# Seams of the first block: sums of squares as columns of 128 tokens by four instead of rows

## The reference

```python
def _rmsnorm(x, g):
    x32 = x.astype(jnp.float32)
    y = x32 * lax.rsqrt(jnp.mean(x32 * x32, axis=-1, keepdims=True) + EPS)
    return (y * g.astype(jnp.float32)).astype(x.dtype)

def _sublayer(x, fn, pre_g, post_g, shift, scale, gate, res_w):
    h = _rmsnorm(x, pre_g) * (1.0 + scale[:, None, :]) + shift[:, None, :]
    y = _rmsnorm(fn(h), post_g)
    return x + res_w * (1.0 + gate[:, None, :]) * y
```

## Time and profile before

| | |
|---|---|
| time, median of 3 runs | 3290.32 us (3289.46 to 3294.41) |
| the profiled execution: its time, its span | 3285.37 us, 3283.4 us |
| mean granted clock of TensorE in it | 0.974 of full speed |
| TensorE busy | 3067.9 us, 93% |
| VectorE busy | 1704.8 us, 52% |
| ScalarE busy | 1162.4 us, 35% |
| GpSimd busy | 1353.0 us, 41% |
| DMA | 365.34 MB, mean 111 GB/s |

### The profile page before, as it was taken

The page is one execution under the profiler, slowest core; times in us unless marked ns, Lnnn a source line. Parts: engine busy times, 40 slices in busy tenths (PEclk is TensorE's granted clock), DMA queues, the critical chain, the costliest instruction groups (busy, mean ns, idle before and its releaser), DMA issues. The chain is left out here.

```text
span 3283.4 us, 52437 instructions
## 1 busy us (share of the span) xinstructions
PE 3067.9 (93%) x20043; PEld 2472.1 (75%) x20043; DVE 1704.8 (52%) x3192; ACT 1162.4 (35%) x2085; POOL 1353.0 (41%) x895
## 2 busy tenths in 40 slices
PE   5999999899999999999999999998888899879997
PEld 4888876688887888877788888876666676668875
DVE  6444478654445575133774116446777756263343
ACT  3222234432223222234422224254454434343442
POOL 3444442344444434442434443245666630323332
PEclk8999999999999999999999999998999999979998
DMA  7665431255544654332354333123222233122221
GB/s 214 195 185 164 156 87 58 67 171 181 181 154 136 187 169 128 95 89 65 111 171 129 97 108 122 51 76 100 55 58 61 60 96 113 33 75 72 74 61 45
DMA packets 636933, 365.34 MB, mean 111 GB/s; under 512 B 107454, under 2 KB 629300, under 8 KB 636240
## 3 DMA queue, kind: packets, MB, share of 16 engines
q1 hardware_dynamic: 628944, 351.42, 36.2%
q10 hardware_dynamic: 6640, 10.49, 1.1%
q0 software_dynamic: 1168, 0.91, 0.1%
HBM read 333.67 MB, written 24.90 MB: 109 GB/s over the span
## 5 line engine op out<-in xcount | busy, mean ns | idle before, releaser
L270 POOL TENSOR_TENSOR w_lo<-w_raw,w_hi 128x1024 fp32r<-128x1024 f32 (+1 forms) x373 | 882.9, 2367 | 1568.3 <-ACT w_hi L262 1515.6
L262 ACT ACTIVATE w_hi<-w_raw 128x1024 fp32r<-128x1024 f32 (+1 forms) x372 | 386.8, 1040 | 946.1 <-PE acc L335 687.9
L335 PE MATMUL acc<-h,w_hi 128*128 128x512 f32 x2256 | 704.6, 393 | 0.0
L335 PEld LDWEIGHTS acc<-h,w_hi 128*128 128x128 f32 x2256 | 417.3, 188 | 84.8 <-issue 1.8
L335 PE MATMUL acc<-h,w_lo 128*128 128x512 f32 x1128 | 440.4, 390 | 0.0
L335 PE MATMUL acc<-hid,w_hi 128*128 128x512 f32 x1056 | 326.6, 390 | 0.0
L1005 DVE SCALAR_TENSOR_TENSOR ada_part<-ada_raw,c_act,ada_part 128x256 f32<-128x256 f32 x672 | 314.9, 488 | 18.6
L335 PE MATMUL lat<-h,w_hi 128*128 128x512 f32 x768 | 276.9, 403 | 16.7 <-DVE h L506 10.4
L335 PEld LDWEIGHTS acc<-h,w_lo 128*128 128x128 f32 x1128 | 211.7, 188 | 45.8
L335 PEld LDWEIGHTS acc<-hid,w_hi 128*128 128x128 f32 x1056 | 197.3, 188 | 40.7
L335 PE MATMUL spare<-h,w_hi 128*128 128x512 f32 x688 | 211.8, 389 | 0.0
(11 more groups left out here) (620 smaller groups left out, 5819.7 us busy)
## 6 DMA issues: line engine op xcount, KB each, us to landing
w_raw<-in_ffn_w SPq DMA_DIRECT2D x240, 512.0 KB, 4.0
ada_raw<-in_ada_w SPq DMA_DIRECT2D x88, 1024.0 KB, 5.0
w_raw<-in_od_w_in SPq DMA_DIRECT2D x32, 512.0 KB, 4.0
w_raw<-in_ffn_w SPq DMA_DIRECT2D x32, 384.0 KB, 3.2
w_raw<-in_ev_w_in SPq DMA_DIRECT2D x22, 512.0 KB, 3.9
image<-inverse_wait SPq DMA_DIRECT2D x144, 64.0 KB, 2.2
first_ada<-in_ada_w SPq DMA_DIRECT2D x8, 1024.0 KB, 12.5
w_raw<-in_ab_w_in SPq DMA_DIRECT2D x16, 512.0 KB, 4.0
```

Source lines behind the costliest of these rows:

```text
L262: act.activation(K.w_hi[:, first % SPLIT, 0:tiles, :], K.raw[:, first % RAW, 0:tiles, :], ACT.Copy).then_inc(K.hi_ready, 1)
L270: pool.tensor_tensor(K.w_lo[:, first % SPLIT, 0:tiles, :], K.raw[:, first % RAW, 0:tiles, :], K.w_hi[:, first % SPLIT, 0:tiles, :].bitcast ...
L335: mm = pe.matmul(out, w[:, slot, k, :], moving(ap, k, tokens), start=first and k == 0 and p == 0, stop=last and k == tiles - 1 and p == le ...
```

## The change

In all seams of the first block and at its start, the sums per token become columns. The data are now the stationary operand and one column of ones (or of factors) moves, so that 128 tokens come out along the partitions, and four such columns hold all 512. The root, the reciprocal, the five operations that follow and `K.x_sums`, `K.root_next` shrink from 128x128 to 128x4. `spread_rows` becomes `spread_columns`: the broadcast column is stationary and the identity moves. In `quick_pre_dve` the step of block 1 moves from ahead of the first `scaled` to behind it; with it `own(1)` and the step of block 2 come behind `low(0)`.

```diff
+def column_sums_pe(pe, K, out, src, start, stop, weights=None):
+    weights = weights if weights is not None else K.ones[:, 0:1]
+    for c in range(4):
+        mm = pe.matmul(out[:, c:c + 1], src[:, c * P:(c + 1) * P], weights, start=start and c == 0, stop=stop and c == 3)
+    return mm
+
+def spread_columns(pe, K, out, columns, ready):
+    pe.wait_ge(ready, 1)
+    for c in range(4):
+        mm = pe.matmul(out[:, c * P:(c + 1) * P], columns[:, c:c + 1].broadcast_to([P, P]), K.ident, start=True, stop=True)
+    return mm
...
-def spread_rows(pe, K, out, rows, ready):
-    pe.wait_ge(ready, 1)
-    for c in range(4):
-        mm = pe.matmul(out[:, c * P:(c + 1) * P], K.ident[:, 32 * c:32 * c + 1].broadcast_to([P, P]), rows[:],
                        start=True, stop=True)
     return mm
...
         own(0)
-        step(1)
         dve.wait_ge(S.factors, 1)
     for b in range(DB):
         scaled(b)
         if update:
+            if b == 0:
+                step(1)
+                low(0)
+                own(1)
+                step(2)
+                continue
             if b + 2 < DB:
                 step(b + 2)
             low(b)
-            if b == 0:
-                own(1)
...
-    act.activation(K.root[:], S.tp[0][:, 0:P], ACT.Sqrt, scale=1.0 / D, bias=K.eps).then_inc(S.post.std_ready, 1)
+    act.activation(K.root[:, 0:4], S.tp[0][:, 0:4], ACT.Sqrt, scale=1.0 / D, bias=K.eps).then_inc(S.post.std_ready, 1)
...
-    sums_pe(pe, K, S.tp[0], K.ssq, True, False)
-    sums_pe(pe, K, bank, S.ssqz, True, False)
-    sums_pe(pe, K, S.tp[1], S.cross, True, False)
+    column_sums_pe(pe, K, S.tp[0], K.ssq, True, False)
+    column_sums_pe(pe, K, bank, S.ssqz, True, False)
+    column_sums_pe(pe, K, S.tp[1], S.cross, True, False)
     pe.wait_ge(S.post.sq_ready, DB)
-    sums_pe(pe, K, S.tp[0], K.sq[:, last % 2], False, True).then_inc(S.post.ssq_done, 1)
-    sums_pe(pe, K, bank, K.sq[:, last % 2], False, True, K.fac[:, 1, last:last + 1].broadcast_to([P, 32]))
+    column_sums_pe(pe, K, S.tp[0], K.sq[:, last % 2], False, True).then_inc(S.post.ssq_done, 1)
+    column_sums_pe(pe, K, bank, K.sq[:, last % 2], False, True, K.fac[:, 1, last:last + 1])
     pe.wait_ge(S.crossed, DB)
-    sums_pe(pe, K, S.tp[1], K.sq[:, 1 - last % 2], False, True).then_inc(S.cross_done, 1)
+    column_sums_pe(pe, K, S.tp[1], K.sq[:, 1 - last % 2], False, True).then_inc(S.cross_done, 1)
     run_on(pe, K, spare, 3)
-    spread_rows(pe, K, K.sums, K.root, S.post.rstd_ready)
+    spread_columns(pe, K, K.sums, K.root, S.post.rstd_ready)
...
-    dve.reciprocal(K.root[:], K.root[:]).then_inc(S.post.rstd_ready, 1)
-    step = K.root_next[:]
+    inverse, step = K.root[:, 0:4], K.root_next[:]
+    dve.reciprocal(inverse, inverse).then_inc(S.post.rstd_ready, 1)
...
-    math(dve.tensor_tensor(step, bank[:, 0:P], K.root[:], ALU.mult))
+    math(dve.tensor_tensor(step, bank[:, 0:4], inverse, ALU.mult))
...
-                    mm = sums_pe(pe, K, sums, S.y[:, b], b == 0, b == DB - 1)
+                    mm = column_sums_pe(pe, K, sums, S.y[:, b], b == 0, b == DB - 1)
                 mm.then_inc(S.x_summed, 1)
-                spread_rows(pe, K, K.spare, K.root_next, S.root_inv)
+                spread_columns(pe, K, K.spare, K.root_next, S.root_inv)
...
-            K.x_sums = sbuf(first, "x_sums", [P, P])
-            K.root_next = sbuf(first, "next_roots", [P, P])
+            K.x_sums = sbuf(first, "x_sums", [P, 4])
+            K.root_next = sbuf(first, "next_roots", [P, 4])
```

More of the change, by code:

```diff
@@ L633, in spread_pe @@
         mm = pe.matmul(K.sums[:, c * P:(c + 1) * P], K.ident[:, 32 * c:32 * c + 1].broadcast_to([P, P]), K.root[:],
-                       start=True, stop=True)
-    return mm
-def spread_rows(pe, K, out, rows, ready):
-    pe.wait_ge(ready, 1)
-    for c in range(4):
-        mm = pe.matmul(out[:, c * P:(c + 1) * P], K.ident[:, 32 * c:32 * c + 1].broadcast_to([P, P]), rows[:],
                        start=True, stop=True)
@@ L679, in quick_pre_pe @@
     run_on(pe, K, spare, 6)
-    spread_rows(pe, K, K.spare, K.root_next, S.next_inv).then_inc(S.factors, 1)
+    spread_columns(pe, K, K.spare, K.root_next, S.next_inv).then_inc(S.factors, 1)
     run_on(pe, K, spare, 6)
@@ L830, in border_dve @@
     dve.wait_ge(S.post.rstd_ready, 1)
-    math(dve.tensor_tensor(step, bank[:, 0:P], K.root[:], ALU.mult))
-    math(dve.scalar_tensor_tensor(step, S.tp[1][:, 0:P], 2.0, step, ALU.mult, ALU.add))
-    math(dve.tensor_tensor(step, step, K.root[:], ALU.mult))
+    math(dve.tensor_tensor(step, bank[:, 0:4], inverse, ALU.mult))
+    math(dve.scalar_tensor_tensor(step, S.tp[1][:, 0:4], 2.0, step, ALU.mult, ALU.add))
+    math(dve.tensor_tensor(step, step, inverse, ALU.mult))
     math(dve.scalar_tensor_tensor(step, K.x_sums[:], -1.0, step, ALU.mult, ALU.max))
@@ L1094, in _ @@
                 act.wait_ge(S.x_summed, 1)
-                act.activation(K.x_sums[:], sums[:, 0:P], ACT.Copy)
-                act.activation(K.root_next[:], sums[:, 0:P], ACT.Sqrt, scale=1.0 / D, bias=K.eps).then_inc(S.root_ready, 1)
+                act.activation(K.x_sums[:], sums[:, 0:4], ACT.Copy)
+                act.activation(K.root_next[:], sums[:, 0:4], ACT.Sqrt, scale=1.0 / D, bias=K.eps).then_inc(S.root_ready, 1)
                 split_hi(act, K, u0, 0, 0, 0, 8)
```

## The result

The changed kernel takes 3320.0 us (median of 4 runs, 3318.6 to 3326.3) against 3289.9 of the kernel before (4 runs): a ratio of 1.0095, 95% interval 1.0081 to 1.0109. It is 30 us slower. The profiled execution took 3318.9 us, its span is 3317.1, 33.7 more than before.

A forecast was written before the change was run, and what follows sets the result against it. TensorE, busy 93% of the span, was taken as the bound. Loads 13.4, behind the phase change 1.4, start 1.2 and clock 21.8 sum to 37.8 us; on the median's scale (3290.3) 3328 us, range 3300 to 3345.

The forecast's parts named there:

- The loads: In six seams, 48 loads of 128 columns at 0.11 us each make TensorE end the phase: +13.4 us.
- The clock: In the seams, one-column matmuls do not hold the full clock, so following loads take twice as long: +21.8 us in six.
- The skill's rule: In the seams, a TensorE kept busy keeps full clock, so the sum would lack 21.8 us; the forecast sided against it.
- Behind the phase change: Head of the next phase: spreading gains 0.3 us, VectorE's order costs 0.66; net +0.34 in four seams, +1.4 us.
- The order: Head of the phase on VectorE: the step of block 2 pushes block 1 and all that follow by 0.66 us.
- The start: At the kernel's start, 64 loads replace 64 narrow ones and the reciprocal is 0.77 us shorter: +1.2 us (-4.2 to +2.8).
- my two cases: At the start: clock falls 2.7 us after the last wide matmul, +2.8 us; or never falls, -4.2 us.
- Faster: Rival: in the seams column groups pass as quickly as row groups (0.2 us), VectorE ends the phase: -7, 3283; chance 0.06.
- The clock holds: Rival: in the seams one-column matmuls count as work and keep the clock: about +13 us, 3303; chance 0.22.

The follow-up runs named there:

- wide: The changed kernel with 128 equal columns moving over the same loaded data instead of one: 3298.2 us, ratio 1.0035 to the kernel before.
- narrow_vector: The kernel before, row sums and TensorE untouched, with a seam's reciprocals and five VectorE operations on 4 columns only (norms not computed): 3284.8 us, 0.9981.
- old_order: The changed kernel with VectorE's order in the head of the phase put back as before: 3317.7 us, ratio 1.0094 to the kernel before.
- warm_start: The kernel before with filler matmuls added at the start, behind the sums, between one-column sums and ahead of the first product: 3286.0 us, 0.9985.
- wide_old_order: The changed kernel with 128 equal columns moving and VectorE's old order: 3296.5 us, ratio 1.0016 to the kernel before.

## Why the prediction was right

Forecast 3328 us (3300 to 3345), measured 3320.0. The two large terms were right in kind and nearly in size. The whole came out 8 us high, mostly by a small term: the forecast added 37.8 us, the profile shows 29.4 at the first product behind the last seam, made of 14.3 for the loads (forecast 13.4), 20.0 for the clock (21.8), -4.3 behind the phase changes (+1.4) and -0.6 at the start (+1.2). The medians differ by 30. Step by step:

1. **The loads.** A group was to take 0.88 us; it takes 0.89 to 0.90 at the full clock. Six seams were to be 13.4 us longer; at a held clock (`wide`) they are 14.4 longer. The difference is in the 7.4 us a seam, which are 7.5 to 7.6. The bound is the one named: TensorE's spreading ends the phase, VectorE is done before it. The seam was to last at least 7.4 us, and by the changed kernel's own windows 9.4 to 12.3, since the low clock came earlier than forecast.
2. **The clock.** The term was 21.8 us (its own items, 3.7 us of loads a seam, give 22.4; the slip does not matter). Between `wide` and the changed kernel lie 14.9 us up to the phase change and 5.0 behind it, 19.9. (The medians differ by 22, but of that 2.8 us arise at the start.) The conclusion from the one stretch at 0.50 held. Its split was wrong: I had the whole low clock behind the sums (9 us ahead of the phase change, 12.8 behind it). In fact it comes 1.7 to 5.2 us into the sums, slows the last groups too, and in the seam shown is over before the second spreading (0.97 for its eight loads at 1051.01). That the two errors cancelled to 2 us is luck.
3. **The skill's rule.** By the Trainium skill ("TensorE: Matmul & The Clock Gate", "Why this matters for your kernels") a TensorE kept busy should keep its clock. Here it was busy 9.27 of 9.53 us in a seam with the clock at 0.75; the measurement decides. With 128 moving columns over the same loads (`wide`) the clock stayed at 1.00 in all six seams.
4. **Behind the phase change.** -0.3 us a seam was right at a held clock (2.53 against 2.83). The order was taken at +0.66 us a seam in four seams; it costs 0.25 to 0.49 alone. By these two effects my +1.4 us should have been about -0.3. But the traces show more: to the first product -2.1 us over six seams (`wide` against before), and between first product and next seam the changed kernel gains 2.3 us over five phases where the order alone loses 1.6. So the term is -4.3, the one most in error. The premise that a microsecond lost in a seam reaches the end whole does not quite hold: the phases behind gave some back. Why is open: `wide` shows it too (-1.5), and in `narrow_vector`, which has the narrow operations but sums rows, no phase gains more than 0.3.
5. **The start.** Taken at +1.2 between -4.2 and +2.8. The root came at 43.44, and the reciprocal waited:

```profile
32.21 9.37 PEld L627 LDWEIGHTS sums<-const,z 128*128 128x128 f32 x64
...
43.18 0.26 ACT L1107 ACTIVATE next_roots<-sums,const 128x4 f32<-128x4 f32 x1
...
43.47 0.18 DVE L1172 RECIPROCAL next_roots<-next_roots 128x4 f32<-128x4 f32 x1 [0.68 <-ACT next_roots L1107]
...
37.00:38.00 1.00, 1.00 (x7) 1.00 (x6) 0.93 (x3) 0.00 (x0) 0.00 (x0) 0.52 1.20 291
```

The clock fell at about 37, between my two cases, and the spreading starts 0.1 us later than before. The first seam even starts 0.6 us earlier than before; so the term is -0.6 and not +1.2. Four profiled kernels with this same start have their first seam at 431.26 to 432.71, so its size is known to a microsecond at best.

6. **The rivals.** "Faster" had as its condition a group under 0.4 us. Groups took 0.89. Its gain, 7 us, was a fair price of the narrow operations: `narrow_vector` measured 6. "The clock holds", at 3303, is the `wide` kernel: 3298 by its median, 3301 by its ratio on 3290. Its profile is 7.3 us behind before at the first product behind the last seam, where that case had 13. The start is not the reason: its first seam starts 3.3 us earlier than before, within the 0.8 to 4.2 of that case (and 1.3 to 3.4 earlier in the three others with this start that have no fillers there). It is again the term behind the phase change: -2.1 to the first products and -1.5 in the phases in place of +1.4.

## What to carry to other kernels

A sum over partitions by matmul costs what it loads: with the data as the stationary operand every 128 columns are loaded, twice in fp32, and on an engine that is the bound this buys short operations on VectorE with long ones on TensorE. Count the loads first. Here a stretch of one-column matmuls lost the clock in all six seams, though TensorE counts as busy all through it; if the form is needed, try letting more columns move over the same loads, which was free here (0.90 us a group either way) and kept it. And where a change makes one side of a seam faster, read who closes it: of 1.4 us taken off VectorE, TensorE let 0.6 to 1.0 through.

## What the runs showed of the hardware

Three groups of one-column matmuls lost the full clock in each of six seams, as six groups did; in the changed kernel's seam at 646 it was gone 1.7 us after the first of them. The low clock then lasted from 3.4 to 10.2 us, in seams whose programs are alike, so that a seam can come out three microseconds longer or shorter for no edit to it: the third takes 9.53 us in the changed kernel and 12.3 in `old_order`, which has the same program there.

The same code takes different times. From the first product behind the last seam on, the programs are the same but for VectorE's order in the head of that phase (in the changed kernel TensorE waits 0.80 us for block 1 there, 0.32 before). That part of the span differs from the kernel before by -2.1 (`warm_start`), +2.4 (`wide`), +4.3 (the changed kernel), +5.5 (`narrow_vector`) and +9.7 us (`wide_old_order`). Windows over the whole of it, before, changed kernel and `wide_old_order`:

```profile
1990.97:3283.40 1292.43, 1157.07 (x10960) 924.08 (x10960) 692.74 (x1327) 528.43 (x1233) 536.57 (x503) 0.95 0.26 72
2020.41:3317.10 1296.69, 1156.67 (x10960) 922.74 (x10960) 689.93 (x1328) 528.65 (x1233) 536.27 (x502) 0.95 0.26 72
1999.89:3302.00 1302.11, 1165.42 (x10960) 929.94 (x10960) 692.96 (x1327) 529.47 (x1233) 535.87 (x503) 0.94 0.26 71
```

In `wide_old_order` TensorE is busy 8.4 us longer with the same matmuls, at a mean clock of 0.94: there most of the 9.7 us goes with the clock. In the changed kernel it is busy 0.4 us less than before, so its 4.3 us are waits of TensorE and not the clock; half a microsecond is the order, the rest is open. For edits worth less than 5 us the shift at a fixed instruction says more here than the time of the whole.
